# Both project stages of a transformer kernel, with another order of loads, splits and tiles at their front

## The reference

```python
def second_block(x, c, positions, norm_w, ada_w, ada_b, w_in, ...):
    c_act = jax.nn.silu(c)
    for l in range(DEPTH):                                   # DEPTH = 2
        shift, scale, gate = jnp.split(c_act @ ada_w[l] + ada_b[l], 3, axis=-1)
        h = rms_norm(x, norm_w[l]) * (1.0 + scale[:, None, :]) + shift[:, None, :]
        proj = h @ w_in[l]                                   # 1024 x 1024 x 2736
        ret_p, mla_p, gla_p = split_cols(proj, ...)
        ...                                                  # retention, latent attention, gated linear attention
        x = x + gate[:, None, :] * (mixed @ w_out[l])
    return rms_norm(x, final_norm)

# the last step of the first block, which the first projection takes over from the experts:
#   ffn = sum over a token's two experts of gate * y[row];  h = layer_norm(ALPHA * h + ffn, ln_g, ln_b)
```

## Time and profile before

| what | value |
|---|---|
| median of 3 runs | 3607.46 us |
| profiled execution, its span | 3608.5 us, 3606.6 us |
| PE busy, DVE, ACT, POOL | 3428.8 us (95%), 2410.1 (67%), 1873.4 (52%), 430.8 (12%) |
| granted TensorE clock, mean | 0.98 |
| DMA, mean | 212 GB/s |
| products of the project stages (L318 to L320) | 286.7 + 282.9 + 282.9 us |
| the row copies of the project stages (L2855) | 96, mean 540 ns |

### The profile page before, as it was taken

How to read it: one execution, slowest core, us unless ns; L and a number is a source line. 1 busy time by engine, 2 the same in 40 slices (tenths; PEclk the granted TensorE clock), 3 DMA queues, 4 the chain that set the end, 5 groups by cost and what they waited for, 6 DMA issues and landing times. The chain is left out here.

```text
span 3606.6 us, 53860 instructions
## 1 busy us (share of the span) xinstructions
PE 3428.8 (95%) x18205; PEld 2678.3 (74%) x18205; DVE 2410.1 (67%) x3983; ACT 1873.4 (52%) x3187; POOL 430.8 (12%) x499
## 2 busy tenths in 40 slices
PE   8998889899999989998999999899999999999988
PEld 7885658688888845686888887477887768787866
DVE  3226877699998957647999888664077655416776
ACT  3215662288888821114888887232167633215764
POOL 0000002011111130000111111410000310000032
PEclk9999999899999999998999999999999999999999
DMA  6643225299999976544999998643242333424142
GB/s 242 227 149 95 71 79 187 93 384 388 378 373 377 360 268 245 199 176 164 381 384 378 378 371 328 235 150 137 72 124 75 128 131 131 168 72 127 43 159 70
DMA packets 416290, 766.17 MB, mean 212 GB/s; under 512 B 107609, under 2 KB 166641, under 8 KB 414072
## 3 DMA queue, kind: packets, MB, share of 16 engines
q1 hardware_dynamic: 393080, 711.93, 55.3%
q0 software_dynamic: 22752, 50.93, 3.8%
q10 hardware_dynamic: 288, 1.05, 0.1%
HBM read 643.00 MB, written 152.72 MB: 221 GB/s over the span
## 5 line engine op out<-in xcount | busy, mean ns | idle before, releaser
L253 DVE TENSOR_TENSOR experts_gate_lo<-weights_gate,experts_gate_hi 128x1024 fp32r<-128x1024 f32 x256 | 301.5, 1221 | 71.5 <-ACT experts_gate_hi L249 71.1
L253 DVE TENSOR_TENSOR experts_down_lo<-weights_down,experts_down_hi 128x1024 fp32r<-128x1024 f32 x256 | 296.2, 1219 | 34.2 <-ACT experts_down_hi L249 34.2
L249 ACT CAST experts_gate_hi<-weights_gate 128x1024 fp32r<-128x1024 f32 x256 | 255.7, 1056 | 110.3 <-DMA weights_gate<-in_moe_w_gate_dram 75.2
L253 DVE TENSOR_TENSOR experts_up_lo<-weights_up,experts_up_hi 128x1024 fp32r<-128x1024 f32 x256 | 295.9, 1218 | 0.3
L318 PE MATMUL project_acc<-project_wh,project_hh 128*128 128x512 f32 (+2 forms) x768 | 286.7, 373 | 0.0
L320 PE MATMUL project_acc<-project_wh,project_hl 128*128 128x512 f32 (+2 forms) x768 | 282.9, 368 | 0.0
L319 PE MATMUL project_acc<-project_wl,project_hh 128*128 128x512 f32 (+2 forms) x768 | 282.9, 368 | 0.0
L249 ACT CAST experts_up_hi<-weights_up 128x1024 fp32r<-128x1024 f32 x256 | 256.0, 1057 | 11.1 <-DMA weights_up<-in_moe_w_up_dram 9.3
L249 ACT CAST experts_down_hi<-weights_down 128x1024 fp32r<-128x1024 f32 x256 | 253.8, 1053 | 6.9 <-DMA weights_down<-in_moe_w_down_dram 6.8
L2855 ACT COPY project_row<-project_acc 128x512 f32<-128x512 f32 (+2 forms) x96 | 51.8, 540 | 365.8 <-PE project_acc L320 365.8
L318 PE MATMUL experts_gp<-experts_gate_hi,experts_xh 128*128 128x512 f32 x512 | 202.4, 395 | 10.9 <-DVE experts_xl L253 10.9
(11 more groups left out here) (560 smaller groups left out, 8190.9 us busy)
## 6 DMA issues: line engine op xcount, KB each, us to landing
weights_gate<-in_moe_w_gate_dram SPq DMA_DIRECT2D x256, 512.0 KB, 11.9
weights_up<-in_moe_w_up_dram SPq DMA_DIRECT2D x256, 512.0 KB, 13.2
weights_down<-in_moe_w_down_dram SPq DMA_DIRECT2D x256, 512.0 KB, 11.4
scratch_y<-qkv_zero SPq DMA_DIRECT2D x48, 512.0 KB, 4.4
pool_shared<-in_ada_w_dram SPq DMA_DIRECT2D x16, 1536.0 KB, 7.9
scratch_proj<-project_row SPq DMA_DIRECT2D x64, 256.0 KB, 2.0
head_store<-in_attn_w_qkv_dram SPq DMA_DIRECT2D x48, 256.0 KB, 3.5
scratch_qkv<-qkv_row SPq DMA_DIRECT2D x48, 256.0 KB, 2.0
```

The costliest lines, as they stand in the source:

```text
L249: return act.copy(hi, src)
L253: return dve.tensor_tensor(lo, src, hi.bitcast(F32), ALU.subtract)
```

## The change

Both fronts are put in another order. No arithmetic is added or taken away, nor is a transfer, but that the raw weights of piece 0 come in two halves with a semaphore each.

```diff
@@ SP @@
-                def load_raw(s):
+                def load_raw(s, part=slice(0, KC), sem=raw_in):
 ...
                 if cb is None:
+                    load_raw(0, slice(0, KC // 2), raw_half_in)
                     load_x(0)
                     load_mods()
+                    load_raw(0, slice(KC // 2, KC))
                     load_x(1)
-                    load_raw(0)
+                    sp.wait_ge(raw_in, 16)
                     sp.dma_start(tab_sb[:, :, :, :], tabs).then_inc(tab_in, 16)
                     load_small()
 ...
                 else:
-                    load_raw(0)
+                    load_raw(0, slice(0, KC // 2), raw_half_in)
+                    sp.wait_ge(cb.y_in[0], 32)
                     load_mods()
+                    load_raw(0, slice(KC // 2, KC))
                     sp.dma_start(tab_sb[:, :, :, :], tabs).then_inc(tab_in, 16)
 ...
@@ POOL, stage A @@
-                        if i + cb.YB < TILES:
+                        if 0 < i and i + cb.YB < TILES:
                             cb.gather(pool, i + cb.YB)
-                        if i < TILES:
-                            cb.power(pool, i)
-                        if i > 0:
-                            mean_power(i - 1)
+                        cb.power(pool, i)
+                        mean_power(i)
+                        if i == 0:
+                            cb.gather(pool, cb.YB)
@@ PE @@
                 if cb is None:
-                    keep_warm(nc, K, lp[:, 0, :], 7)
+                    keep_warm(nc, K, lp[:, 0, :], 12)
                     transposes(0)
-                    keep_warm(nc, K, lp[:, 0, :], 7)
+                    keep_warm(nc, K, lp[:, 0, :], 3)
                 else:
-                    keep_warm(nc, K, acc[:, AB - 1, :], 8)
-                    for i in range(4):
+                    for i in range(2):
+                        keep_warm(nc, K, acc[:, AB - 1, :], 8 - 3 * i)
                         cb.sums(nc, pe, i)
                     keep_warm(nc, K, acc[:, AB - 1, :], 6)
                     transposes(0)
-                    cb.sums(nc, pe, 4)
-                    keep_warm(nc, K, acc[:, AB - 1, :], 3)
-                    transposes(1)
+                    keep_warm(nc, K, acc[:, AB - 1, :], 2)
                 for s, t, n in steps:
-                    if cb is None and s == 0 and t + 1 < TILES:
+                    if cb is None and s == 0 and 0 < t < TILES - 1:
                         transposes(t + 1)
+                    if cb is not None and s == 0 and t + 2 < TILES:
+                        cb.sums(nc, pe, t + 2)
 ...                                  # the product of (s, t)
-                    if cb is not None and s == 0:
-                        if t + 5 < TILES:
-                            cb.sums(nc, pe, t + 5)
-                        if t + 2 < TILES:
-                            transposes(t + 2)
+                    if s == 0 and (t == 0 or cb is not None and t + 1 < TILES):
+                        transposes(t + 1)
@@ ACT, inside the loop, stage A @@
+                        if t == TILES - 3:
+                            for k in range(KC):
+                                w_his(1, k)
 ...                                  # the row copy of tile t
+                    if s == 0 and cb is not None:
+                        if t + 1 < TILES:
+                            h_his(t + 1)
+                        if t + 2 < TILES:
+                            square(t + 2)
@@ DVE, inside the loop, stage A @@
-                        if t + 4 < TILES:
-                            cb.add(dve, cch, t + 4)
-                        if t + 3 < TILES:
-                            norm(t + 3)
+                        if t + 2 < TILES - 1:
+                            cb.add(dve, cch, t + 2)
+                        if t + 1 < TILES:
+                            make_h(t + 1)
+                        if t + 2 == TILES - 1:
+                            cb.add(dve, cch, t + 2)
                         if t + 2 < TILES:
-                            make_h(t + 2)
+                            norm(t + 2)
+                        if t + 2 == TILES:
+                            for k in range(KC // 2):
+                                w_los(1, k)
                         if t + 1 < TILES:
                             h_los(t + 1)
```

More of the change, by code:

```diff
@@ L2609, in split_at @@
             if cb is not None and s == 0:
[L2610 removed]
+                return []
             return split_turn(t)
@@ L2821, in _ @@
                 if cb is None:
+                    for k in range(KC // 2):
+                        w_his(0, k)
                     square(0)
-                    square(1)
-                    for k in range(KC):
+                    for k in range(KC // 2, KC):
                         w_his(0, k)
                     h_his(0)
+                    square(1)
                 else:
@@ L2829, in _ @@
                     cb.diagonals(act, 1)
-                    for k in range(KC):
+                    for k in range(KC // 2):
                         w_his(0, k)
                     cb.diagonals(act, 2)
-                    cb.diagonals(act, 3)
+                    for k in range(KC // 2, KC):
+                        w_his(0, k)
                     square(0)
-                    cb.diagonals(act, 4)
+                    h_his(0)
                     square(1)
-                    h_his(0)
-                    cb.diagonals(act, 5)
-                    square(2)
                 for s, t, n in steps:
-                    if s == 0:
-                        if cb is not None and t + 6 < TILES:
-                            cb.diagonals(act, t + 6)
+                    if s == 0 and cb is not None:
+                        if t + 3 < TILES:
+                            cb.diagonals(act, t + 3)
+                        if t == TILES - 3:
+                            for k in range(KC):
+                                w_his(1, k)
+                    elif s == 0:
                         if t + 1 < TILES:
                             h_his(t + 1)
-                        ahead = 2 if cb is None else 3
-                        if t + ahead < TILES:
-                            square(t + ahead)
+                        if t + 2 < TILES:
+                            square(t + 2)
                     j = latent_tile(s, t)
@@ L2946, in _ @@
                 if cb is None:
+                    for k in range(KC // 2):
+                        w_los(0, k)
                     dve.wait_ge(mod_in, 32)
                     make_h(0)
-                    make_h(1)
-                    for k in range(KC):
+                    for k in range(KC // 2, KC):
                         w_los(0, k)
                     h_los(0)
+                    make_h(1)
                 else:
@@ L3002, in _ @@
                         w_los(s + 1, k)
+                    if cb is not None and n == TILES - 2:
+                        for k in range(KC // 2, KC):
+                            w_los(1, k)
                     j = latent_tile(s, t)
```

47 lines of the change are left out of this document (23 added, 24 removed).

## The result

The changed kernel is slower: median 3614.42 us (3609.18 to 3625.58, 13 runs) against 3608.41 (3605.31 to 3613.27, 13 runs of the kernel before beside them). The ratio is 1.0020, 95% interval 1.0013 to 1.0027: +7.2 us (4.7 to 9.7). The forecast was 3605.2 with a range of 3597 to 3612.

What follows compares the result with a forecast made beforehand. TensorE, busy 95% of 3606.6 us, was taken as the bound, so a front counts only by its waits. First project stage -4.7 plus second +2.4 gave -2.3: 3606.2, or 3605.2 on the median's scale; range 3597 to 3612.

Steps and rivals of the forecast that it cites:

- First gather: First project stage: the first gather lands at 2272.7 instead of 2277.05, with over 2 MiB less in front of it.
- Landing L: First project stage: second half of the raw weights lands at 2283.5; low end 2280.5, high end 2289.7.
- the prediction's own sign: First project stage: the forecast is wrong if the second weight half lands outside 2281 to 2286.
- The 6.25 MiB of the prediction: First project stage: total of raw weights, modulation rows, tables and three gathers, before and after, used to time the landing.
- L + 16.3: First project stage: product(0) starts 16.3 us after the second half's landing, at 2299.8, 14.6 us earlier than before.
- mean-power(0): First project stage, POOL: 0.19 + 0.56 us with VectorE idle, 0.9 charged; otherwise the sum is 1.0 us later.
- Clock: TensorE: 1.8 us charged wherever it idles about 2 us or more, for the 1.2 GHz level.
- Tail of A: End of the first stage's first piece: 3.1 us idle plus 1.8 clock at product(6), 2.5 instead of 0.8 before product(7).
- A, forecast -4.7: First project stage as a whole: piece ends at 2373.5 instead of 2378.15, -4.7 us; with the landing's ends -7.7 and +1.5.
- Stage B: Second project stage: product(0) 4.1 us earlier, then TensorE waits a 6.35 us chain before transposes(2), clock 1.8; +2.4 us.
- x(2) behind them lands about 2973, before it is wanted at 2976.5: Second project stage: tile x(2), loaded behind tables and small weights, lands about 2973, before it is wanted at 2976.5.
- Rival 1: Second half lands late, at 2289.7: first stage +1.5, second +2.4, together +3.9, 3611.4 us; chance 16%.

Runs made afterwards that it cites:

- a_norm: As a_only, but norm(0), square(0) and make_h(0) go ahead of splitting the second half of the weights; 4.3 us faster than the kernel before.
- a_only: First project stage as in the changed kernel, second as before; -0.4 us against the kernel before (-3.6 to 2.9), median 3605.1.
- a_nowait: As a_only, without the load queue's wait for the first gather; 3605.7 us, -1.1 against the kernel before (-4.7 to 2.5).
- b_nowait: As b_only, without the load queue's wait for the second half of the weights; second project stage 308.0 us long in its trace.
- b_only: First project stage as before, second as in the changed kernel; 5.4 us slower than the kernel before (2.2 to 8.7).
- a_warm: As a_norm, with 6 warm-up matmuls on TensorE ahead of its wait for h_los(6) and 3 ahead of h_los(7); -7.6 us against the kernel before.
- a_best: As a_warm, with 4 and 2 warm-up matmuls instead of 6 and 3; 7.9 us less than the kernel before.
- best: First stage of a_best; second with weight halves, transposes(1) ahead of product(0), x(2) loaded ahead of the queue's wait; -9.0 us against the kernel before.
- best2: First stage of a_best; second with weight halves, transposes(1) ahead of product(0), no queue wait for the second half; -10.1 us against the kernel before.

## Why the prediction was wrong

**First gather.** Forecast 8.2 us after the stage's start (2272.7), measured 8.8. Right.

**Landing L, the step that failed in A.** Forecast 19.0 after the start, measured 22.0 in the changed kernel and 21.5 to 23.1 in the six others that wait for the gather: inside the bound of 25.2, but 2.5 to 4 late. By the prediction's own sign (2281 to 2286, that is 16.5 to 21.5 after the start) L was outside, counted from the stage's start. The term was mis-sized: I counted 3 MiB between the half's issue and its landing (mods, half, gather 2). The windows view of that stretch shows 4 MiB (341 GB/s for 12.4 us):

```profile
2269.80:2282.20 12.40, 12.40 (x30) 5.51 (x29) 2.94 (x6) 0.70 (x2) 2.16 (x4) 1.00 0.94 341
```

The DMA view of the same stretch has SP's queue and POOL's side by side (packets, MB, share of the 16 engines):

```profile
q1 hardware_dynamic: 1057, 2.74, 62.5%
q0 software_dynamic: 409, 1.47, 31.2%
```

POOL's queue moved 1.40 MiB, so 0.4 of gather 1, still under way, besides gather 2. SP's moved 2.61 MiB, 0.6 more than mods and half: that can only be the tables and the residual tile, which were issued behind the half (2270.26 and 2273.48) and landed 0.7 and 1.9 us after it. The 6.25 MiB of the prediction had left the residual tile out, and it took the tables to come after the half. An estimate: 1 MiB at 341 GB/s is 3.1 us, which is what L is late by.

The Trainium skill (DMA: Bandwidth & Descriptors, Queues, rings and completion order) says that an engine takes turns between queues that have work; the trace agrees in that both queues moved data in this stretch and neither was served first. The error was in the bytes, not in the sharing.

**L + 16.3.** Measured 2298.2 - 2282.25 = 16.0. Right, mean-power(0) too (0.19 + 0.55 us with VectorE standing still). a_norm shows it to be the dear part: half of it was work that could be done before L.

**Clock.** The 1.8 us behind every idle of about 2 us were read from one trace. The idle of 1.9 us of the earlier trace rows stands in all nine traces with the old stage A: in five of them transposes and product behind it took 8.1 us, in four 6.5. The price was one that an execution may or may not pay.

**Tail of A.** Idles of 3.1 and 2.5 - 0.8 = 1.7 were forecast, 3.22 and 1.61 measured. The clock's 1.8 behind the first was 2.8 in a_only, 1.6 in a_norm, 1.4 in a_nowait, and nothing in the changed kernel's trace. A, forecast -4.7, was -2.7 in that trace and -0.4 (-3.6 to 2.9) by a_only's times. L's 3 us are shown; that the clock is what differs between -2.7 and -0.4 rests on one trace of each.

**Stage B, the step that failed there:** "transposes(2) at 2975.3 + 6.35 = 2981.65 ... Stage B: +2.4". The chain was right (6.30), but two sizes ahead of it and behind it were not. The second half was forecast to land 12.8 us after the start ("2966.63 - 1.35 = 2965.3") and landed at 13.9 (14.2 before), so the head start of product(0) was 3.0, not 4.1; and the clock cost 2.3, not 1.8. Together that is +4.0 at transposes(3) in place of +2.4. By times it is 5.4 (2.2 to 8.7). One reason can be seen: the kernel before, against whose trace this is counted, had the low clock in its own product(0). Its transposes(3) start at 34.9, in the five other traces with the old stage B at 33.1 to 34.9, so the 38.9 of the changed kernel are 4.0 to 5.8 late.

"x(2) behind them lands about 2973, before it is wanted at 2976.5" is 20.5 and 24.0 us after the start. It landed at 24.9 and was wanted at 25.5: the second half of the sentence came true by 0.7 us, because the chain was late too. I had costed the queue's wait at nothing. Taking it away alone gained nothing (b_nowait against b_only), but it ate every repair of the chain.

**Sum.** -2.3 forecast; a_only and b_only give -0.4 + 5.4 = +5.0, within the 4.7 to 9.7 of the whole change. The two traces alone give -2.7 + 4.0 = +1.3: how the rest comes about in the executions that were not traced is known only as far as a_only's and b_only's times split it. Rival 1 (L late, +3.9 in all) came nearest in its sum, but by luck: it has +1.5 in A and +2.4 in B, the runs -0.4 and +5.4.

## What to carry to other kernels

A stage's first tile sets nothing if the second waits: write down for each of the first three tiles the last of its releasers and the one before it, since a repair of one only uncovers the other. A wait put into a load queue stops everything behind it, also loads that are wanted far later by the order but soon by the clock of the stage; put first what is wanted first, and no wait. Where an in-order engine must stand for a transfer, all work that doesn't need it goes ahead of it, and a gap on TensorE that can't be closed is filled with matmuls no longer than the gap.

## What the runs showed of the hardware

The same idle of 3.2 us ahead of product(6) was followed by the 1.2 GHz level for a time in a_only (0.65 over nine us), a_norm (7.2 us for the product) and a_nowait (7.0), and not in the changed kernel (5.6). The Trainium skill (TensorE: Matmul & The Clock Gate, Part 1: The HAM clock gate) says that the clock depends on how busy the array has been and that the same kernel can come out differently from run to run; these traces agree. With the gap filled the product took 5.6 to 5.9 us in all four kernels (a_warm, a_best, best, best2), and the clock stayed at 1.00.

The last mixing section, identical in all kernels, lasted 167.6 to 173.5 us in 17 traces; the two ends are b_only and best2, and I see no relation to what was changed. A single pair of traces can't carry a difference of some us, here not even its sign.
